# First weight pair of the seven-product part of each feed-forward: loads and sums issued at other points

## The reference, cut to what matters

```python
def swiglu(x, w1, w3, w2):
    return (jax.nn.silu(x @ w1) * (x @ w3)) @ w2
...
h = x + (0.5 * swiglu(rmsnorm(x, p['ffn1_norm']), p['ffn1_w1'], p['ffn1_w3'], p['ffn1_w2'])).astype(x.dtype)
...
h = h + (0.5 * swiglu(rmsnorm(h, p['ffn2_norm']), p['ffn2_w1'], p['ffn2_w3'], p['ffn2_w2'])).astype(x.dtype)
```

## Time and profile before

| | |
|---|---|
| median of 3 runs | 1250.4 us (1249.78 to 1251.92) |
| profiled execution | 1251.1 us, of which the span from the first to the last instruction is 1249.3 us |
| PE busy | 1208.6 us, 97% of the span |
| DVE, ACT, POOL busy | 64%, 41%, 10% |
| chain that ended last | PE 84%, DVE 8%, DMA 2% |
| mean granted TensorE clock | 0.987 of full |

### The profile page before, as it was taken

The page is one execution under the profiler, slowest core; times in us unless marked ns, Lnnn a source line. Parts: engine busy times, 40 slices in busy tenths (PEclk is TensorE's granted clock), DMA queues, the critical chain, the costliest instruction groups (busy, mean ns, idle before and its releaser), DMA issues.

```text
span 1249.3 us, 23502 instructions
## 1 busy us (share of the span) xinstructions
PE 1208.6 (97%) x9703; PEld 1154.5 (92%) x9703; DVE 794.7 (64%) x1241; ACT 515.6 (41%) x838; POOL 127.2 (10%) x156
## 2 busy tenths in 40 slices
PE   7999999999999999999989999999999999999995
PEld 7999999999999989998757998689999999999995
DVE  6888888863336528765786532444878888883322
ACT  6354455542222233355855321433444445462211
POOL 0021111000001000044310011000011111100000
PEclk9999999999999999999999999999999999999997
DMA  4388777433333212222675356712278777533321
GB/s 161 108 217 197 178 185 180 110 101 93 93 94 130 85 51 85 73 90 67 203 245 175 102 182 231 292 51 84 61 198 203 180 178 182 148 99 92 91 59 69
DMA packets 63189, 169.47 MB, mean 136 GB/s; under 512 B 7233, under 2 KB 7425, under 8 KB 60657
## 3 DMA queue, kind: packets, MB, share of 16 engines
q1 hardware_dynamic: 46656, 118.22, 30.2%
q0 software_dynamic: 16144, 49.29, 16.4%
q10 hardware_dynamic: 288, 0.53, 0.1%
HBM read 158.96 MB, written 9.06 MB: 134 GB/s over the span
## 4 chain that ended last, share of the span: by engine, by line
PE 84%; DVE 8%; DMA 2%; issue 2%; ACT 2%; POOL 0%; SPq 0%; POOLq 0%; DVEq 0%; ACTq 0%
PE ps L469 26%; PE ps L470 25%; PE ps L471 25%; DMA raw<-in_w_up 2%; DVE w_lo L432 1%; PE ps L2231 1%; PE ps L2169 1%; ACT w_hi L422 1%; PE ps L1379 1%; PE ps L565 1%; DVE sq_sum L549 1%; PE ps L594 0%; DVE xs_lo L783 0%; PE ps L2323 0%; PE ps L2132 0%
## 5 line engine op out<-in xcount | busy, mean ns | idle before, releaser
L469 PE MATMUL ps<-xs_lo,w_hi 128*128 128x260 f32 x1008 | 285.5, 283 | 4.4 <-DVE xs_lo L783 3.9
L470 PE MATMUL ps<-xs_hi,w_lo 128*128 128x260 f32 x1008 | 286.2, 284 | 0.0
L471 PE MATMUL ps<-xs_hi,w_hi 128*128 128x260 f32 x1008 | 285.6, 283 | 0.0
L471 PE MATMUL ps<-x_hi,w_hi 128*128 128x260 f32 (+1 forms) x896 | 255.1, 285 | 0.0
L470 PE MATMUL ps<-x_hi,w_lo 128*128 128x260 f32 (+1 forms) x896 | 254.7, 284 | 0.0
L432 DVE TENSOR_TENSOR w_lo<-raw,w_hi 128x1024 fp32r<-128x1024 f32 (+1 forms) x132 | 157.5, 1195 | 151.7 <-ACT w_hi L422 145.4
L469 PE MATMUL ps<-x_lo,w_hi 128*128 128x260 f32 (+1 forms) x832 | 243.3, 292 | 6.7 <-DVE xf L1100 2.1
L422 ACT ACTIVATE w_hi<-raw 128x1024 fp32r<-128x1024 f32 (+1 forms) x128 | 130.8, 1026 | 211.6 <-PE ps L471 173.4
L725 ACT ACTIVATE w_hi<-raw 128x512 fp32r<-128x512 f32 x234 | 139.3, 626 | 168.2 <-DVE raw L744 134.3
L469 PE MATMUL ps<-gu_lo,w_hi 128*128 128x260 f32 x704 | 198.8, 282 | 1.6 <-DVE join L856 1.6
L469 PEld LDWEIGHTS ps<-xs_lo,w_hi 128*128 128x128 f32 x1008 | 190.7, 189 | 5.1 <-DVE xs_lo L783 4.3
(11 more groups left out here) (362 smaller groups left out, 1773.2 us busy)
## 6 DMA issues: line engine op xcount, KB each, us to landing
raw<-in_w_up SPq DMA_DIRECT2D x162, 256.0 KB, 3.5
raw<-in_w_down SPq DMA_DIRECT2D x32, 512.0 KB, 3.6
raw<-in_w_up POOLq DMA_DIRECT2D x54, 256.0 KB, 5.6
cache<-in_cache POOLq DMA_DIRECT2D x11, 1024.0 KB, 9.2
raw<-in_w_up SPq DMA_DIRECT2D x16, 512.0 KB, 3.5
raw<-in_w_down SPq DMA_DIRECT2D x16, 384.0 KB, 3.1
v_early<-in_cache POOLq DMA_DIRECT2D x5, 1024.0 KB, 9.8
z<-in_w_up SPq DMA_DIRECT2D x18, 256.0 KB, 2.7
```

What stands on the lines that cost most here:

```text
L469: nc.tensor.matmul(out, w_h, m_l, start=start, stop=False)
L470: nc.tensor.matmul(out, w_l, m_h, start=False, stop=False)
L471: return nc.tensor.matmul(out, w_h, m_h, start=False, stop=stop)
```

## The change

The first pair of each feed-forward gets a loading order of its own (`first_win_loads`). Quarter 4 is loaded right behind the issue of the last plain unit's weights, without a wait, and POOL adds to it as soon as it has landed, by itself. Quarters 0 and 1 are loaded when unit 6's raw weights are split, quarter 2 and then 3 when unit 7's are; POOL adds to quarter 2 behind that. The waits that counted both loads or both sums at once now count the first one where only the first is read (`both_or_first`), and a few waits are added so that increments of one semaphore can't be taken for one another: on SP ahead of quarters 2 and 3, on POOL ahead of the second sum, and on SP ahead of the third pair's quarters 4 (until both sums of the first pair have landed) and 1 (until ACT has read a22 of the first pair). Nothing is computed otherwise, and no instruction of PE, ACT or DVE is moved.

```diff
+        def both_or_first(f, i):
+            return 32 * (f * (WIN // 2) + i // 2 + 1) - (16 if i == 0 else 0)
...
             elif name in ("a12", "a22"):
-                nc.scalar.wait_ge(rest_loaded[i % 2], 32 * loads)
+                nc.scalar.wait_ge(rest_loaded[i % 2], both_or_first(f, i) if name == "a12" else 32 * loads)
             elif name in ("s1", "s3"):
-                nc.scalar.wait_ge(z_added[i % 2], 32 * loads)
+                nc.scalar.wait_ge(z_added[i % 2], both_or_first(f, i) if name == "s1" else 32 * loads)
...
             if name == "s2":
-                nc.vector.wait_ge(z_added[i % 2], 32 * (f * (WIN // 2) + i // 2 + 1))
+                nc.vector.wait_ge(z_added[i % 2], both_or_first(f, i))
...
+        def first_win_loads(gate, lin, f, up):
+            one = 32 * f * (WIN // 2) + 16
+            nc.sync.dma_start(quarter(0, 4), lin[:, 0:QUART]).then_inc(z_loaded[0], 16)
+            nc.sync.wait_ge(w_lo, up.u0 + up.units - 1)
+            nc.sync.dma_start(quarter(0, 0), gate[:, 0:QUART]).then_inc(a11_loaded[0], 16)
+            nc.sync.dma_start(quarter(0, 1), gate[:, QUART:]).then_inc(rest_loaded[0], 16)
+            nc.sync.wait_ge(w_lo, up.u0 + up.units)
+            nc.sync.wait_ge(z_loaded[0], one)
+            nc.sync.dma_start(quarter(0, 2), gate[:, 0:QUART]).then_inc(z_loaded[0], 16)
+            nc.sync.wait_ge(rest_loaded[0], one)
+            nc.sync.dma_start(quarter(0, 3), lin[:, QUART:]).then_inc(rest_loaded[0], 16)
...
                 if i == 0:
-                    nc.sync.wait_ge(w_lo, up.u0 + up.units)
-                elif i == 1:
+                    first_win_loads(gate, lin, f, up)
+                    continue
+                if i == 1:
                     nc.sync.wait_ge(unit_done, up.u0 + up.units)
...
+                if i == 2:
+                    nc.sync.wait_ge(z_added[0], both_or_first(f, 0) + 16)
                 free("s1")
...
+                if i == 2:
+                    nc.sync.wait_ge(f_hi, f * NFORM + FORM_AT["a22", 0] + 1)
                 nc.sync.dma_start(quarter(i, 1), gate[:, QUART:]).then_inc(rest_loaded[i % 2], 16)
...
-                nc.gpsimd.wait_ge(z_loaded[i % 2], 32 * (f * (WIN // 2) + i // 2 + 1))
+                nc.gpsimd.wait_ge(z_loaded[i % 2], both_or_first(f, i))
                 nc.gpsimd.dma_start(quarter(i, 4), lin[:, QUART:], accum_op=ALU.add).then_inc(z_added[i % 2], 16)
+                if i == 0:
+                    nc.gpsimd.wait_ge(z_loaded[0], both_or_first(f, 0) + 16)
+                    nc.gpsimd.wait_ge(z_added[0], both_or_first(f, 0))
                 nc.gpsimd.dma_start(quarter(i, 2), lin[:, 0:QUART], accum_op=ALU.add).then_inc(z_added[i % 2], 16)
```

## The result

| | before | after |
|---|---|---|
| median of 16 runs | 1249.93 us (1246.4 to 1253.89) | 1256.22 us (1253.71 to 1259.5) |
| ratio, with its 95% interval | | 1.005 (1.0039 to 1.0061) |
| profiled execution, span | 1251.1, 1249.3 us | 1259.5, 1257.7 us |
| mean granted TensorE clock in it | 0.987 | 0.982 |

The change made the kernel 6.3 us slower, outside the range. The profiled execution of after is the slowest of its 16 runs, so its rows can show more of the loss than the median holds.

The account below looks back on a forecast made before the run. PE was taken as the bound, through 84% of the span, with waits at the border from plain units to pairs. First feed-forward 0 + 1.55, second -2.07, together -0.5 us, gave 1249.9 us, range 1246.5 to 1253.5.

Parts of the forecast that it names:

- The waits for the first pair's sum go; PE starts 1.72 and 2.53 us sooner.: Border from plain units to pairs: DVE's 3.27 and 4.21 us waits go, so PE's first form starts sooner.
- PE then runs eight forms and stops at a12 of the second pair.: After the first form: one PE stop of about 2.3 and 1.9 us idle; gains 0 and 2.07 us.
- The price that no row shows: Landing of the second pair's second accumulate beside earlier third-pair loads: 1.7 us sooner to 2.2 later possible, no change taken.
- already hold the press of those loads: Second pair's second accumulate: its 7.46 us landing, against the usual 5.8, was read as already including the third pair's loads.
- nothing of it moves: Chain to a12 of the second pair: its first load still waits for the last plain unit's end, at the same time.
- the forecast of no measurable change: Whole kernel: together -0.5 us, 1249.9 us; 0.68 chance of a time within 0.2% of before.
- The clock: 1.55 us behind the first stop, nothing behind the second.: Behind the new stops at a12 of the second pair: 1.55 us charged in the first feed-forward, none in the second.
- The slower rival: Third pair's earlier loads delay the second pair's accumulate up to 1.7 and 2.2 us, clock falls twice: +4.9, 1255.3; chance 0.13.
- beyond sharing: DMA queues: engines take turns, so SP's longer queue does not hold up POOL's accumulates more than sharing; sum stays.
- the high end by order of arrival: Second pair's second accumulate: four loads go ahead, 3.4 us on top of 5.8, so 1.7 and 2.2 us later.

Follow-up runs that it names:

- e5: Kernel before, with the third pair's quarters 0, 1 and 3 held until both sums of the second pair have landed: 1248.48 us, ratio 0.9989.
- e6: Changed kernel, third pair's quarters 2, 0, 1 and 3 held until the remainder of a11 of the second pair is made: 1251.61 us, ratio 1.0008.
- e7: Changed kernel, third pair's quarters 4 and 2 held until PE did six forms, 0, 1 and 3 until the second pair's sums landed: 1245.56 us.
- e1: Changed kernel, third pair's quarters 0, 1 and 3 held until both sums of the second pair have landed: 1247.82 us, ratio 0.9988.
- e2: Changed kernel, all five loads of the third pair held until both sums of the second pair have landed: 1251.99 us, ratio 1.0017.
- e9: e7 with the second pair's quarters 4 and 2 loaded after five of eight activation tiles of the last plain unit: 1247.09 us.
- e11: e7 plus 6 matmuls that compute nothing on PE ahead of a12 of the second pair: 1245.05 us, ratio 0.9971.
- e8: e1 plus 10 matmuls that compute nothing on PE ahead of a12 of the second pair: 1248.04 us, ratio 0.9987.
- e3: Changed kernel plus 28 matmuls that compute nothing on PE ahead of a12 of the second pair: 1254.22 us, ratio 1.0036.
- e4: Changed kernel, third pair's accumulates held on POOL until both of the second pair's have landed, loads left as they are: 1254.85 us, ratio 1.0043.
- e12: e1 with the second pair's quarters 4 and 2 loaded after five of eight activation tiles of the last plain unit: 1245.42 us.
- e10: Changed kernel, second pair's quarters 4 and 2 loaded after five of eight activation tiles of the last plain unit, no hold: 1246.32 us.

## Why the prediction was wrong, step by step

- **The waits for the first pair's sum go; PE starts 1.72 and 2.53 us sooner.** Right. The last blend's remainder ended 1.52 and 1.96 us ahead of the slot; forecast were 1.6 and 1.7.
- **PE then runs eight forms and stops at a12 of the second pair.** Right: it was there 11.70 us behind the slot in both feed-forwards (11.6 forecast), and DVE line 730, now 734, ended the stop. (In the second feed-forward the prediction writes the wait from 927.2 to 929.27 as 2.1 us; from 927.26, its own sum, it is 2.0. Nothing else rests on it.)
- **The price that no row shows: "I take no change".** This is the step that failed. The argument was that the accumulates "shared the engines with the same loads before, and the same bytes are due by the same time". Before, one load of the third pair was issued ahead of the second accumulate; now five were, and its landing took 1.4 and 1.6 us longer. The reading that the 7.46 us "already hold the press of those loads" is not borne out: with three of them held in the kernel before (e5) it took 6.96 and 7.50. The accumulate was issued later too, by 0.3 and 1.0 us, where the prediction had "nothing of it moves"; the third pair's loads do not explain that part (e6, e7), and its cause stays open. The result landed 1.6 and 2.5 us later than forecast: the first feed-forward lost 1.6 in place of nothing, the second lost 0.4 in place of gaining 2.07. e1, e2 and e7 shorten the landing by moving the third pair's loads alone. With four of them back near their old place (e6) the forecast of no measurable change holds for the time, but its stops, 3.4 and 3.6 us, are not the forecast ones, so that agreement is partly luck.
- **The clock: 1.55 us behind the first stop, nothing behind the second.** Wrong in size, as a consequence: the stops were 4.0 and 4.5 us long, and in the profile the clock fell behind both and for twice as long, 2.6 and 2.4 us, against 1.55 before. On the median the clock costs some 3.5 us more than before, by the estimate above, where the forecast had it even.
- **The slower rival was the case that came true.** The place and the mechanism are as written, and both waits did exceed 3.5 us with a fall of the clock behind each. It had +1.7 and +0.1 us for the start of a12 of the second pair, measured were +1.6 and +0.4; and it had 3.1 for the clock behind the two new stops, where the profile shows 5.0. Its sum of +4.9 stands against +6.3 on the median. It was given 0.13. The evidence for it, 1 MB that moves ahead of the accumulates, stood in the order of instructions and outweighed the sentence that was set against it.

The Trainium skill ("DMA: Bandwidth & Descriptors", section "Queues, rings and completion order") has each DMA engine take turns between the queues that have work. From it the prediction read that SP's longer queue would not hold up POOL's accumulates "beyond sharing". The landings of 8.83 and 8.58 us lie between the forecast 7.46 and 7.03 and the high end by order of arrival, 9.2 in both. The rule is not contradicted, and its use was wrong: by it five queued loads take their turns beside the accumulate where one did, and the sharing would then itself be the cost. No run here shows the order of the packets.

The Trainium skill ("TensorE: Matmul & The Clock Gate", section "HAM oscillation — how this bites in real kernels") lets the clock fall behind gaps longer than any that the forecast held. It fell behind the 4.0 and 4.5 us here, which agrees; but it fell behind 2.03 (e1), 1.90 (e7) and 1.80 us (e2) of idle time too, which does not.

## What to carry to other kernels

A wait that is taken away does not only start an engine sooner: it frees buffers sooner, and the loads that they were waiting for are issued sooner, here into the one transfer that the next stop hangs on. So list, for each transfer on the path, which others are issued ahead of it before and after the change; where that number grows, take a longer landing as the likely case, not the unlikely one. Hold loads with time to spare behind the urgent transfer, but only those: held too long (e2, e9) they are the next stop.

## What the runs showed of the hardware that was not expected

- The second pair's second accumulating DMA, of 256 KB, landed in 5.25 to 5.83 us with no load of the third pair issued ahead of it (e2, e7, e11), in 6.96 to 7.97 with one (before, e5, e6), in 5.55 to 7.23 with two (e1, e8), in 7.96 to 9.73 with all five (the change, e3, e4). How near they stand counts too: with the second pair sooner it took 6.2 to 7.0 us with the third pair's loads held in two steps (e9), 7.9 to 8.95 with two of them issued within 0.8 us of it (e12).
- At the border, the clock fell to half behind all six stops of 1.8 to 2.4 us (before, e1, e2, e7, e10) for 3.4 us, behind the six of 3.4 to 4.6 us for 6.8 us (the change, e4, e6) or 3.4 us (e6), and was not seen to fall behind stops of 1.6 us and less.
- The same instructions at the start of the program ran at half clock for 3.4 us in some executions and for 6.8 in others, worth some 1.6 us, so one profile against one profile can be off by that.
